# Splits between the maxima and the scaling of probabilities, and one reciprocal for two heads

## The reference

```python
# latent tokens: per head, row and block of 16 columns, 8 rows x 32 keys of the window and 256 cached keys
s_loc = einsum(q_r, kb) * scale + bias          # masked outside the window
s_ctx = einsum(q_r, ck) * scale
p = softmax(concatenate([s_loc, s_ctx], axis=-1), axis=-1)
out = einsum(p_loc, vb) + einsum(p[..., n_loc:], cv)
# prompt tokens: softmax(q k^T * scale) v over 128 keys, for each head
```

## Time and profile before

| | |
|---|---|
| median of 3 runs | 561.96 us |
| the profiled execution's own time | 562.78 us |
| its span in the profile | 560.9 us |
| PE busy | 513.3 us (92%) |
| DVE busy | 442.5 us (79%) |
| ACT busy | 272.8 us (49%) |
| POOL busy | 103.1 us (18%) |

### The profile page before, as it was taken

One profiled execution on the slowest core, in us unless ns is written; L12 is line 12 of the kernel. 1 busy time (PEld: TensorE's weight loads), 2 busy tenths in 40 slices (PEclk: granted clock), 3 DMA queues, 4 the chain that ended last, 5 costly groups with the idle time before them and its releaser, 6 DMA issues.

```text
span 560.9 us, 8109 instructions
## 1 busy us (share of the span) xinstructions
PE 513.3 (92%) x3142; PEld 421.7 (75%) x3142; DVE 442.5 (79%) x720; ACT 272.8 (49%) x378; POOL 103.1 (18%) x114
## 2 busy tenths in 40 slices
PE   4999999999999997888999999999999999999670
PEld 1679999997899995666787787877888887777220
DVE  3216999989799406998559878979999988897895
ACT  2327502021221316887612215559888887784363
POOL 0005700012000001221000000213534242412301
PEclk9999999999999999999999999999999999999786
DMA  8997996629786622128099119649999999968567
GB/s 299 387 386 227 236 354 206 226 78 296 265 282 242 183 46 57 40 58 240 24 331 328 55 45 366 249 130 332 382 388 390 402 380 385 377 255 313 218 232 161
DMA packets 55743, 138.17 MB, mean 246 GB/s; under 512 B 8311, under 2 KB 17074, under 8 KB 49816
## 3 DMA queue, kind: packets, MB, share of 16 engines
q1 hardware_dynamic: 43704, 114.87, 57.8%
q0 software_dynamic: 9120, 20.80, 12.8%
q10 hardware_dynamic: 2880, 1.98, 1.2%
HBM read 127.61 MB, written 18.10 MB: 260 GB/s over the span
## 4 chain that ended last, share of the span: by engine, by line
PE 48%; DVE 25%; DMA 12%; issue 8%; ACT 5%; POOL 0%; DVEq 0%; SPq 0%; POOLq 0%; ACTq 0%
DMA uni<-in_w_expert_out 9%; PE PS L1872 7%; PE PS L1873 7%; PE PS L1877 7%; PE PS L1774 5%; PE PS L1776 5%; PE PS L1775 5%; DVE uni L1212 4%; DVE act_lo L1520 2%; PE PS L1801 2%; DMA raw<-in_w_ada 2%; PE PS L2269 2%; DVE PS L1322 1%; PE PS L1794 1%; ACT act_hi L991 1%
## 5 line engine op out<-in xcount | busy, mean ns | idle before, releaser
L1774 PE MATMUL PS<-w_hi,act_hi 128*128 128x512 f32 x256 | 103.6, 405 | 1.6 <-DVE act_lo L1541 0.9
L1776 PE MATMUL PS<-w_hi,act_lo 128*128 128x512 f32 x256 | 100.1, 391 | 0.0
L1775 PE MATMUL PS<-w_lo,act_hi 128*128 128x512 f32 x256 | 99.9, 390 | 0.0
L1872 PE MATMUL PS<-act_hi,w_hi 128*128 128x320 f32 x320 | 97.5, 313 | 0.2 <-issue 0.2
L1873 PE MATMUL PS<-act_lo,w_hi 128*128 128x320 f32 x320 | 96.4, 309 | 0.0
L1212 DVE SCALAR_TENSOR_TENSOR uni<-raw,uni 128x512 f32<-128x512 f32 x112 | 75.3, 747 | 1.3 <-DMA raw<-in_w_ada 1.3
L1877 PE MATMUL PS<-act_hi,w_lo 128*128 128x320 f32 x320 | 72.9, 309 | 0.0
L1448 DVE TENSOR_TENSOR w_lo<-raw,w_hi 128x2048 fp32r<-128x2048 f32 x28 | 64.0, 2285 | 1.0 <-ACT w_hi L981 0.7
L1872 PEld LDWEIGHTS PS<-act_hi,w_hi 128*128 128x128 f32 x320 | 60.1, 188 | 4.0 <-issue 2.8
L1873 PEld LDWEIGHTS PS<-act_lo,w_hi 128*128 128x128 f32 x320 | 60.1, 188 | 0.0
L1774 PEld LDWEIGHTS PS<-w_hi,act_hi 128*128 128x128 f32 x256 | 48.1, 188 | 13.6 <-issue 2.7
(11 more groups left out here) (274 smaller groups left out, 874.6 us busy)
## 6 DMA issues: line engine op xcount, KB each, us to landing
raw<-in_w_expert_in SPq DMA_DIRECT2D x28, 1024.0 KB, 12.7
raw<-in_w_ada SPq DMA_DIRECT2D x20, 1024.0 KB, 7.4
uni<-in_w_expert_out SPq DMA_DIRECT2D x16, 1024.0 KB, 11.3
raw<-in_w_in SPq DMA_DIRECT2D x12, 1024.0 KB, 9.8
uni<-expert_rows SPq DMA_DIRECT2D x10, 512.0 KB, 7.3
uni<-in_w_ada SPq DMA_DIRECT2D x4, 1024.0 KB, 14.6
raw<-in_w_out SPq DMA_DIRECT2D x4, 1024.0 KB, 6.0
w_lo_before_subtraction<-in_w_expert_in SPq DMA_DIRECT2D x4, 1024.0 KB, 7.4
```

The costliest lines, as they stand in the source:

```text
L1774: T.matmul(out, lh, rh, start=first, stop=False)
L1775: T.matmul(out, lh, rl, start=False, stop=False)
L1776: return T.matmul(out, ll, rh, start=False, stop=last)
L1872: T.matmul(out, a, h_hi[:, k, sl], start=f, stop=False)
```

## The change

In VectorE's loop the splits of other data (`last_lo`, `conv_lo`, `mix_lo`) move from behind the scaling of step v to between the maxima and the scaling of step v. The two reciprocals of a step, one for each head, become one of both sums (elements 0 and 4 of the row, with a stride; for the prompt all eight), which waits for the exponentials of both sides. The scalings of both sides follow. Nothing changes on the other engines.

```diff
+            def inverse_sums(v):
+
+                dve.wait_ge(s_p, 2 * v + 2)
+                step = 4 if v < PAIRS else 1
+                link(V.reciprocal(rinv[:, v % 2, 0:8:step], rsum[:, v % 2, 0:8:step]))
+
             def norm_probs(v, side):
 
-                dve.wait_ge(s_p, 2 * v + side + 1)
                 b, c = 2 * (v % 2) + side, 4 * side
                 if v < PAIRS:
-                    link(V.reciprocal(rinv[:, v % 2, c:c + 1], rsum[:, v % 2, c:c + 1]))
                     a = V.tensor_scalar(prob[:, b, :], prob[:, b, :], rinv[:, v % 2, c:c + 1], None, ALU.mult)
                 else:
-                    link(V.reciprocal(rinv[:, v % 2, c:c + 4], rsum[:, v % 2, c:c + 4]))
                     p4 = prob[:, b, :].rearrange("p (j t) -> p j t", j=4)
...
                 if v < NV:
                     bias_and_max(v, 0)
                     bias_and_max(v, 1)
-                    norm_probs(v, 0)
-                    norm_probs(v, 1)
                 if v - 1 in LAST_HI_AT:
                     last_lo(LAST_HI_AT.index(v - 1))
                 if v - 1 in CONV_HI_AT:
                     conv_lo(CONV_HI_AT.index(v - 1))
                 if v >= 7 and (v - 7) % NB == 0 and v - 7 < PAIRS - NB:
                     mix_lo((v - 7) // NB)
+                if v < NV:
+                    inverse_sums(v)
+                    norm_probs(v, 0)
+                    norm_probs(v, 1)
```

## The result

The changed kernel takes 559.33 us (median of 8 runs, 557.57 to 561.0), the kernel before 562.78 us (8 runs, 561.93 to 564.45). The ratio worked out from the runs is 0.9929 with a 95% interval of 0.9913 to 0.9946, that is 4.0 us less (3.0 to 4.9); the plain difference of the two medians is 3.45. In a second round of runs on another occasion it was 559.18 against 562.71, ratio 0.9932 [0.9906, 0.9958]. The forecast was 558.0 for a median before of 561.96, a gain of 4.0.

The account below looks back on a forecast made before the run. VectorE's in-order queue was taken as nearest to full in the attention, whose values product times all that follows. Shorter steps gain 3.6 to 4.15, taken as 4.0: 561.96 to 558.0 us, range 556.9 to 560.2.

Parts of the forecast that it names:

- no split: Attention steps 0, 1, 12, 13, 14, without a split on VectorE: 3.27 us each, 0.40 more than before.
- small split: Attention steps with a convolution split (6, 8, 9, 10) or result split (7, 11, 15): 3.27 us, 0.40 less than before.
- weight split: Attention steps 2 to 5, with 1.14 us of split: 3.40 us each, 0.60 less than before.
- the low end of that bound: Weight steps last 3.40 us if the split starts with the second maximum's accumulator read, 3.54 if after it.
- Step 16: The attention's last step, the prompt: its first maximum at 266.66 us, where before it was 271.09.
- TensorE's 0.05: Smallest slack in the attention steps: scores ready every 3.21 us, under VectorE's 3.27; all fit by 0.05 to 0.3.
- Rival 1: Attention transposes wait for the first head, steps 3 to 15 each 0.25 us longer: gain 0.8, 561.2 us; chance 0.10.
- rival 3: Step 13's bias windows land late beside SyncE's modulation loads: 1 us at worst seen, 564 at 14 us landing; chance 0.04.
- Rival 2: Behind the attention, expert weight transfers meet others differently and half the gain goes: 560.0 us; chance 0.10.

Follow-up runs that it names:

- the move alone: The changed kernel with the splits moved but a reciprocal for each head as before: 559.26 us, ratio 0.9937 to the kernel before.
- The merge alone: The changed kernel with one reciprocal for both heads but the splits behind the scaling as before: 567.90 us, ratio 1.0086 to the kernel before.

## Why the prediction was right

*The time.* 559.33 lies 1.3 above the forecast of 558.0 and within the range of 556.9 to 560.2. Of the 1.3, 0.8 is the median of the kernel before, which came out at 562.78 in eight runs where three had given 561.96. That the ratio gives exactly the 4.0 that was forecast is finer than its interval (3.0 to 4.9), and so luck; the step lengths bear the forecast out more closely.

*The step lengths.* Predicted 3.27, 3.27 and 3.40 (no split, small split, weight split); measured 3.26 to 3.27, 3.26 to 3.27, 3.38 to 3.42. The instruction behind the second maximum does start with the accumulator's read (+1.26, 226.01 - 224.75), so the low end of that bound was the right one. The reciprocal of two takes 0.17 us instead of 0.16, of eight 0.20. The gap of about 0.2 us that was expected before the reciprocal in the steps with a small split is 0.12 (in step 7 the split ends at 240.35, the reciprocal starts at 240.47).

*Step 16.* Predicted 4.43 us earlier (266.66 against 271.09), measured 4.48 from the attention's start. The first three steps came out as reckoned. The merge costs 0.8 in steps 0 and 1; step 2 gives back 0.92 (4.34 to 3.42), 0.6 by its moved split and 0.3 because the longer wait for ScalarE (0.53 before its reciprocal where step 3 had 0.20) is gone. Step 3 starts 9.96 us after step 0 (214.79 to 224.75), predicted 9.94 (213.82 to 223.76), before 10.08.

*Who is next.* ScalarE had less slack than was read for it in the weight steps: in step 3 its weight copy ends at 225.41 and the exponentials start at 225.53, 0.12 us later where 0.2 was reckoned, and they start 0.78 us after the maximum all the same. In no step of the kernel after does VectorE wait for scores, so TensorE's 0.05 was enough. ScalarE's rows of step 3:

```profile
224.35 1.06 ACT L872 ACTIVATE w_hi<-raw 128x1024 fp32r<-128x1024 f32 x1
225.53 0.69 ACT L881 ACTIVATE uni<-PS,small 128x512 f32<-128x512 f32 x1
```

Rival 1 (transposes wait for the first head) did not come: behind step 0 TensorE's waits before the transposes end on ScalarE's copy, as before. The rule that rival 1 leaned on, "breaking up instructions may allow work to be completed sooner" (the Trainium skill, "Perfetto Trace Analysis", section Optimizing Scalar/DVE Operations), is borne out in the steps 0 and 1: there two reciprocals are worth 0.40 us a step (2.87 against 3.27). In the steps 12 to 14 they are worth 0.2 us in all three, since TensorE then sets the pace. The sentence speaks of engines that are not saturated; in the weight steps VectorE is busy 13.47 of 13.61 us, so it says nothing of them, and there the merged reciprocal saves 0.2 us a step.

*The dropped reciprocal's price.* The row's 0.20 us and the Trainium skill's 60 ns ("Perfetto Trace Analysis", section Optimizing Scalar/DVE Operations; an estimate of a gain of 3.4 in all from it) are told apart by the move alone: 3.62 against 3.42 in steps 2 and 3. The row was right: in the path stands the time from the start of the reciprocal to that of the scaling, 0.17 to 0.20 us in the rows of the move alone.

*The bias windows (rival 3).* The condition came true, the loss did not. GpSimd's issues in the kernel after:

```profile
249.69 1.40 POOL L649 DMA_DIRECT2D uni<-bias_windows  x2 [5.12 <-DVE small L1322]
252.96 1.40 POOL L649 DMA_DIRECT2D uni<-bias_windows  x2 [1.86 <-DVE small L1322]
```

SyncE's, of the modulation rows:

```profile
250.21 1.00 SPq L459 DMA_DIRECT2D raw<-mod_rows  x2
```

And the time to landing of the two windows of step 15 (the second row of GpSimd's):

```profile
DMA to landing us min/median/max: 8.0/8.0/8.0
DMA to landing us min/median/max: 9.4/9.4/9.4
```

The windows of step 13 (249.69) took at most 5.3 us, and step 13 starts at 257.79. Those of step 15 took 8.0 and 9.4 us, where the same pair took 5.3 and 7.8 in the kernel before and the longest of all its 24 was 8.4. The later one, issued at 253.5, is there at 262.9, and step 15 wants it at 264.32. So the prediction named the wrong pair; the margin is 1.4 us. How far it could be pushed was not tried. In the seven further traces the longest landing of a window is 8.6 to 9.6 us, and no step waits for one.

*Afterwards.* Rival 2 (part of the gain lost behind the attention) can't be seen: 4.3 us at the values product against 4.0 us end to end with an interval of 3.0 to 4.9. Nor can the traces settle it: from the load issued behind the product to the end of the span they have 280.4 us before and 281.2 after, and 278.9 to 282.6 in the seven further traces, a scatter of 3.7 us, as wide as the gain. The merge alone passed on 4.8 of 5.1, with an interval of 3.3 to 6.4.

What the prediction did not see is how the gain divides. It priced the merge at +0.40 or -0.20 a step but took the sum only for both edits; with the splits moved, the merge's own terms almost cancel, and by the runs it costs 0.2 us in all (52.79 against 52.59).

## What to carry to other kernels

On an engine whose queue runs in order, first look for the wait that its own work released (maxima, exponentials, scaling), and put work on other data into it until it is filled; that is worth more than dropping an instruction. One wait for two results is right only where something covers the later one; without cover it takes away the overlap that the two waits gave, 0.40 us a step in steps 0 and 1 here. When the idle time is filled, read the slack of the other engines in the same step: here 0.05 to 0.3 us by the prediction's working. Where the merge was taken out of steps 12 to 14, VectorE at once waited for scores, so in those steps no more is to be had from VectorE alone.

## What the runs showed of the hardware

An instruction whose semaphore wait stood right behind another wait on VectorE's queue began 0.10 us after its releaser instead of 0.03, at three steps of one kernel. Beside six loads of 512 KB that SyncE issued between 250.2 and 256.4 us, two DMAs of 128 KB took 8.0 and 9.4 us to land, where six that the kernel before issued at 237.6 to 245.6 us took 2.9 to 3.2. That the large loads are the cause was not tried apart.
